# Input projections of a hybrid decoder step as seven products per pair of column blocks, in three passes over the tokens

## The chip, the cores and the metric

The kernel runs on one core of a Trainium2 chip. The metric is the device time of one execution in microseconds (us), the median of three runs. The profile shows one further execution, taken by the hardware profiler.

## The reference, cut to what matters

One layer of a decoder trunk, over 2048 prompt tokens and 8 tokens of running sequences (2056 in all), with 1024 channels, all in float32:

```python
xn = rmsnorm(x, norm_w)
proj = xn @ w_in        # 1024 x 10248
q, k, v, i_pre, f_pre, o_pre, z_m, b_g, c_g, x_c, z_c, g_m, g_c = jnp.split(proj, offs, axis=-1)
h, C1, n1, m1 = mlstm_chunkwise(q, k * DQK ** -0.5, v, ig, lf, C0, n0, m0)   # 4 heads
h = rmsnorm_per_head(h) * sigmoid(o_pre) * silu(z_m)
y_m = h @ w_proj_m
cv, conv1 = short_conv(c_g * x_c, conv0, conv_w)      # width 3, causal
y_c = (silu(z_c) * b_g * cv) @ w_proj_c
out = x + (sigmoid(g_m) * y_m + sigmoid(g_c) * y_c) @ w_out
```

and a final RMS norm. Besides the outputs for both groups of tokens the kernel returns the states of the mLSTM (C, n, m) and the last rows of the convolution.

## The kernel before, in words

Every float32 product is made of three fp32r matmuls: an operand is split into a high part (ScalarE, ACT, copies it to fp32r) and a low part (VectorE, DVE, subtracts), and high x high, high x low and low x high are summed in PSUM.

Phase A (from L128) normalises and transposes x. ACT (`hi`, L261) and DVE (`lo`, L310) split the transposed tile out of PSUM into `RH` and `RL`, which hold all 2056 tokens in SBUF; the v columns and the two gate columns are multiplied there (L365).

Phase B (from L395) makes all other input projections. It takes 36 pairs of column blocks of 128: q and k (4 pairs), o and z (8), then c and x, s and b (16 pairs, two per channel block), gm and gc (8). For each block SyncE's queue (SP) loads 1024 x 128 weights (`load_w`, L514), ACT makes `w_hi` (L751), DVE `w_lo` (L874), and TensorE (PE) runs five tiles of 412 or 410 tokens (`TILES`), each of 24 matmuls, into two PSUM banks in turn (`tile`, L1138 to L1151). ACT or DVE empties each tile (L785, L789, L803, L834, L851, L856; L943, L1035, L1060) into a row of 2056 tokens in SBUF, which SP stores to DRAM. The order of the work is written out by hand, with a semaphore for each step, and every engine's queue runs in order.

The mLSTM's 16 chunks of 128 tokens are spread over the 16 pairs of the convolution stage, one chunk to a pair. A chunk's steps are done between tiles: scores and the transposed k before tile 0 (L1201, L1205), one head before each of tiles 2 to 5 (L1217 to L1219, and on DVE L982 to L990), the normalised h transposed before tile 8 (L1223). The 8 samples' state updates follow in the gm/gc pairs (L1099 to L1108). GpSimd (POOL) does nothing but powers of a few elements (L237, L736, L738, L1603), memsets and masks.

Phases C (L1485) and D (L1675) are the three output projections; they use 294 and 512 columns per matmul. The change leaves their code as it is.

```python
for k in range(KB):
    for w, x in ((WH, g.RH), (WH, g.RL), (WL, g.RH)):
        last = nc.tensor.matmul(G[j % 2][:, 0:n], w[:, par, k, :], x[:, k, c0:c0 + n], ...)
```

Of the kernel before, what the change touches and what calls it, by code (L numbers as in the profile page):

```python
# [45 lines left out]
TILES = [(0, 412), (412, 412), (824, 412), (1236, 410), (1646, 410)]  # L46
NTILE = len(TILES)
# [39 lines left out]
def build(nc, inputs, outputs):  # L87
# [4 lines left out]
    with top:  # L92
        top.enter_context(nc.allow_non_contiguous_dma(reason="small per-channel columns"))
        RH = sbuf(nc, top, "RH", [P, KB, T], F32R)
        RL = sbuf(nc, top, "RL", [P, KB, T], F32R)
# [5 lines left out]
        g.v_rows = dram("v_rows", T, D)  # L101
        g.qT_d = dram("qT_d", NH, P, TP)
# [11 lines left out]
        g.RH, g.RL, g.RHf = RH, RL, RH[:, :, :].bitcast(F32)  # L114
# [5 lines left out]
        g.IF = sbuf(nc, early, "IF", [P, NT, 2 * NH])  # L120
        with early:
            phase_a(nc, g)
            phase_b(nc, g)
        phase_c(nc, g)
        phase_d(nc, g)


def phase_a(nc, g):  # L128
# [7 lines left out]
    xt = [sbuf(nc, ctx, f"xt{j}", [P, D]) for j in range(2)]  # L136
    stage = [sbuf(nc, ctx, f"wv_stage{j}", [P, VW]) for j in range(2)] + [g.S[:, 1], g.S[:, 0]]
# [12 lines left out]
    transposed, hi_set, lo_set = sem("transposed"), sem("hi_set"), sem("lo_set")  # L150
    v_done, v_act, v_dve = sem("v_done"), sem("v_act"), sem("v_dve")
    v_stored = [sem("v_stored0"), sem("v_stored1")]

# [10 lines left out]
    def seen(i, par):  # L164

        return 8 * i + (8 if par else 16)

# [12 lines left out]
    with nc.Block() as block:  # L180

        @block.sync
        def _(sp):
# [22 lines left out]

            def body(i, par):
                if rows(i) == P:
                    sp.wait_ge(transposed, i)
                    load_x(i + 1, 1 - par)  # L210
                if isinstance(i, int) and i == 2:
                    store(0, 0)
                store(i - 1, 1 - par)

            over_tiles(sp, body)

# [26 lines left out]

        @block.scalar
        def _(act):
# [12 lines left out]
            def hi(i):  # L258
                act.wait_ge(transposed, i + 1)
                for j in range(2):  # L260
                    nc.scalar.activation(g.RH[:, 4 * j:4 * j + 4, at(i)], turned(i)[j][:, :, 0:rows(i)], ACT.Copy).then_inc(hi_set, 1)  # L261

# [14 lines left out]
            hi(0)  # L277
            hi(1)
# [4 lines left out]
            def body(i, par):  # L283
                hi(i)
# [10 lines left out]
        def _(dve):  # L295
# [11 lines left out]
            def lo(i):  # L307
                for j in range(2):
                    dve.wait_ge(hi_set, 2 * i + j + 1)
                    nc.vector.tensor_tensor(g.RL[:, 4 * j:4 * j + 4, at(i)], turned(i)[j][:, :, 0:rows(i)],  # L310
                                            g.RHf[:, 4 * j:4 * j + 4, at(i)], ALU.subtract).then_inc(lo_set, 1)
# [18 lines left out]
            lo(0)  # L330
            lo(1)
# [5 lines left out]
            def body(i, par):  # L337
                lo(i)
# [10 lines left out]
        def _(pe):  # L349
# [11 lines left out]
            def block_product(i, j, k):  # L361

                n = rows(i)
                for m, (x, w) in enumerate(((g.RH, WH), (g.RH, WL), (g.RL, WH))):
                    last = nc.tensor.matmul(V[3 * (i % 2) + j][:n, 0:VC], x[:, k, i * P:i * P + n],  # L365
# [29 lines left out]
def phase_b(nc, g):  # L395
# [3 lines left out]
    WS = g.S[:, :, 0:D].rearrange("p a (k n) -> p a k n", k=KB)  # L399
    WH = sbuf(nc, ctx, "w_hi", [P, 2, KB, P], F32R)  # L400
    WL = sbuf(nc, ctx, "w_lo", [P, 2, KB, P], F32R)

    E0 = sbuf(nc, ctx, "row0", [P, TP])
    E1 = sbuf(nc, ctx, "row1", [P, TP])
    ZT = sbuf(nc, ctx, "z_tanh", [P, 2, 412])
    CV = sbuf(nc, ctx, "conv_tile", [P, 412])
# [4 lines left out]
    nM = sbuf(nc, ctx, "negM", [P, NH, P])  # L411
# [20 lines left out]
    ut_rows = [nM[0:2 + NS, :, :].rearrange("p a b -> p (a b)"), ZT[0:2 + NS, :, :].rearrange("p a n -> p (a n)")[:, 0:512]]  # L432
# [13 lines left out]
    G = [psum(nc, ctx, f"b_g{j}", [P, 512]) for j in range(2)]  # L446
    PS = psum(nc, ctx, "b_s", [P, NH, P])
    PT = [psum(nc, ctx, f"b_t{j}", [P, NH, P]) for j in range(2)]
    PN = [psum(nc, ctx, f"b_n{j}", [P, 512]) for j in range(2)]
    PC = psum(nc, ctx, "b_c", [P, 512])  # L450
# [1258 lines left out]
```

## Time and profile before

| what | value |
|---|---|
| three runs | 2554.98, 2556.01, 2557.18 us |
| profiled execution, its own time | 2556.17 us |
| its span in the trace | 2554.4 us |
| granted TensorE clock, mean | 0.995 |
| busy: PE, DVE, ACT, POOL | 99%, 32%, 17%, 2% of the span |
| DMA | 233.92 MB, mean 92 GB/s |

Matmuls are pipelined, so the duration in a matmul's row is longer than the distance from one start to the next; a rate is read as a window's length over its matmuls. The span holds four stretches of PE: phase A to 225.2 us, phase B from 231.1 to 1975.0 us, phase C from 1981.8 us and phase D to the end.

### The profile page before, as it was taken

To read this page: it belongs to the slowest core of one execution; us is meant where nothing else is said; L and a number is where in the kernel's file an instruction comes from. 1 tells how busy PE (TensorE), PEld (TensorE's weight loads), DVE (VectorE), ACT (ScalarE), POOL (GpSimd) and SP (SyncE) were. 2 spreads that over 40 slices of the span, in tenths; PEclk is the share of its full clock that TensorE was granted. 3 is DMA by queue.
4 is the path that set the end of the run, shared out by engine and by line. 5 is a ranking of instruction groups with operands and counts; after the bars stand their busy time and mean duration, and the time that the engine had idled before them with its cause. 6 is when DMAs were issued, how large, how long until landed. Compare 5 with 4: busy or idle time off the path is not lost. (4 is left out here: it accounts for less than half of the span.)

```text
span 2554.4 us, 35363 instructions
## 1 busy us (share of the span) xinstructions
PE 2517.9 (99%) x14265; PEld 2449.2 (96%) x14265; DVE 814.6 (32%) x1415; ACT 435.0 (17%) x806; POOL 43.5 (2%) x66
## 2 busy tenths in 40 slices
PE   7999999999999999999999999999999999999998
PEld 7998999999999999999999999999999999999886
DVE  4331000211213534535345353231212622324333
ACT  3221111111111111121111111111111301001111
POOL 0000000000000000000000000000000000000000
PEclk9999999999999999999999999999999999999999
DMA  4223122121213312233122321252333753335442
GB/s 149 83 83 62 67 82 70 33 66 33 66 33 87 91 53 78 62 91 86 54 78 70 99 70 41 72 147 91 113 109 100 258 159 101 106 94 167 128 148 84
DMA packets 238896, 233.92 MB, mean 92 GB/s; under 512 B 16010, under 2 KB 216970, under 8 KB 233862
## 3 DMA queue, kind: packets, MB, share of 16 engines
q1 hardware_dynamic: 238854, 233.33, 30.1%
q8 instruction: 31, 0.51, 0.1%
q14 instruction: 11, 0.09, 0.0%
HBM read 152.62 MB, written 80.71 MB: 91 GB/s over the span
## 5 line engine op out<-in xcount | busy, mean ns | idle before, releaser
L1148 PE MATMUL b_g<-RH,w_hi 128*128 128x412 f32 (+1 forms) x2880 | 1021.2, 355 | 5.8 <-DVE w_lo L874 5.8
L1148 PE MATMUL b_g<-RL,w_hi 128*128 128x412 f32 (+1 forms) x2880 | 1006.7, 350 | 0.0
L1148 PE MATMUL b_g<-RH,w_lo 128*128 128x412 f32 (+1 forms) x2880 | 1006.1, 349 | 0.0
L1148 PEld LDWEIGHTS b_g<-RH,w_hi 128*128 128x128 f32 x2880 | 542.0, 188 | 9.8 <-DVE w_lo L874 6.1
L1148 PEld LDWEIGHTS b_g<-RL,w_hi 128*128 128x128 f32 x2880 | 541.8, 188 | 4.2
L1148 PEld LDWEIGHTS b_g<-RH,w_lo 128*128 128x128 f32 x2880 | 541.7, 188 | 1.4
L1485 PE MATMUL c_g<-act_hi,RH 128*128 128x294 f32 x896 | 268.4, 300 | 6.7 <-DVE act_lo L1435 6.7
L1485 PE MATMUL c_g<-act_lo,RH 128*128 128x294 f32 x896 | 268.8, 300 | 0.0
L1485 PE MATMUL c_g<-act_hi,RL 128*128 128x294 f32 x896 | 268.6, 300 | 0.0
L874 DVE TENSOR_TENSOR w_lo<-stages,w_hi 128x1024 fp32r<-128x1024 f32 x72 | 88.2, 1225 | 558.8 <-ACT w_hi L751 558.6
L1485 PEld LDWEIGHTS c_g<-act_hi,RH 128*128 128x128 f32 x896 | 169.6, 189 | 7.6 <-issue 7.3
L1485 PEld LDWEIGHTS c_g<-act_lo,RH 128*128 128x128 f32 x896 | 170.1, 190 | 0.0
L1485 PEld LDWEIGHTS c_g<-act_hi,RL 128*128 128x128 f32 x896 | 170.0, 190 | 0.0
L365 PE MATMUL a_v<-wv_hi,RH 128*128 128x344 f32 (+1 forms) x408 | 133.3, 327 | 3.6 <-DVE wv_lo L315 3.2
L751 ACT ACTIVATE w_hi<-stages 128x1024 fp32r<-128x1024 f32 x72 | 76.0, 1055 | 327.8 <-PE b_g L1148 324.9
L365 PE MATMUL a_v<-wv_hi,RL 128*128 128x344 f32 (+1 forms) x408 | 131.7, 323 | 0.0
L943 DVE SCALAR_TENSOR_TENSOR row<-z_tanh,b_g 128x412 f32<-128x412 f32 (+1 forms) x80 | 46.6, 583 | 266.7 <-ACT z_tanh L778 266.7
L365 PE MATMUL a_v<-wv_lo,RH 128*128 128x344 f32 (+1 forms) x408 | 130.9, 321 | 0.0
L1675 PE MATMUL d_g<-RH,mix_hi 128*128 128x512 f32 (+1 forms) x272 | 108.7, 400 | 4.2 <-DVE mix_lo L1617 4.2
L1675 PE MATMUL d_g<-RH,mix_lo 128*128 128x512 f32 (+1 forms) x272 | 108.2, 398 | 0.0
L1675 PE MATMUL d_g<-RL,mix_hi 128*128 128x512 f32 (+1 forms) x272 | 107.7, 396 | 0.0
L778 ACT ACTIVATE z_tanh<-b_g 128x412 f32<-128x412 f32 (+1 forms) x80 | 41.1, 514 | 259.7 <-PE b_g L1148 259.7
(219 smaller groups left out, 1783.0 us busy)
## 6 DMA issues: line engine op xcount, KB each, us to landing
stages<-w_in SPq DMA_DIRECT2D x72, 512.0 KB, 6.0
act_stage<-cv_d SPq DMA_DIRECT2D x7, 1176.0 KB, 12.8
tanh_gate<-tm_d SPq DMA_DIRECT2D x7, 1176.0 KB, 6.0
tanh_gate<-tc_d SPq DMA_DIRECT2D x7, 1176.0 KB, 9.2
mix_d<-mix SPq DMA_DIRECT2D x7, 1176.0 KB, 7.1
gate_d<-row SPq DMA_DIRECT2D x8, 1028.0 KB, 5.6
cv_d<-row SPq DMA_DIRECT2D x8, 1028.0 KB, 5.2
tm_d<-row SPq DMA_DIRECT2D x8, 1028.0 KB, 4.5
```

The costliest lines, as they stand in the source:

```text
L365: last = nc.tensor.matmul(V[3 * (i % 2) + j][:n, 0:VC], x[:, k, i * P:i * P + n], w[:, k, j * VC:(j + 1) * VC], start=(k == 0 and m == 0), ...
L751: nc.scalar.activation(WH[:, par], WS[:, par], ACT.Copy).then_inc(w_hi, 1)
L778: nc.scalar.activation(ZT[:, b, 0:n], G[b][:, 0:n], ACT.Tanh, scale=0.5).then_inc(z_set, 1)
L874: nc.vector.tensor_tensor(WL[:, par], WS[:, par], WH[:, par].bitcast(F32), ALU.subtract).then_inc(w_ready, 1)
L943: nc.vector.scalar_tensor_tensor(out=E1[:, c0:c0 + n], in0=ZT[:, b, 0:n], scalar=1.0, in1=G[b][:, 0:n], op0=ALU.add, op1=ALU.mult).then_in ...
L1148: last = nc.tensor.matmul(G[j % 2][:, 0:n], w[:, par, k, :], x[:, k, c0:c0 + n], start=(step == 0), stop=(step == 3 * KB - 1))
L1485: last = nc.tensor.matmul(G[o % NB][:, 0:TN], w[:, k, c0:c0 + P], x[:, k, :], start=(k == 0 and m == 0), stop=(k == KB - 1 and m == 2))
L1675: last = nc.tensor.matmul(G[2 * par + j][:n, :], x[par][:, k, 0:n], w[:, k, j * N:(j + 1) * N], start=(step == 0), stop=(step == 3 * KB - 1))
```

## The change

In phase B a pair of column blocks and a stretch of 2n tokens are taken as a 2 x 2 by 2 x 2 block product (halves of the 1024 channels, the two column blocks, two token groups of n) and computed with seven block products instead of eight, by sums and differences of quarters. The tokens are taken in three passes with n = 260, 384 and 384; each pass goes through all 36 pairs and loads all their weights. A product is 12 matmuls of n columns; four PSUM banks take the seven products, three of them on top of an earlier one.

POOL makes four sums of 512 elements per partition for each pair. ACT and DVE split seven operands of 512 elements per pair, for the pair that comes next. ACT copies banks 0 out twice per pair, DVE adds five times. `RH` and `RL` are no longer kept in phases A and B: phase A also writes the transposed x to DRAM (`xT_d`), four quarters come back for each pass, and the seven x operands (`x_hi`, `x_lo`, one buffer each) are built anew in each pass. The activations run on whole rows after a pair's last product (`finish`). The stages are now q/k, o/z, gm/gc, convolution; chunks run in all four bodies (two pairs each) of gm/gc and, in passes 2 and 3, in the first two bodies of the convolution. The sample updates move to the q/k and o/z bodies of the second pass.

```diff
-TILES = [(0, 412), (412, 412), (824, 412), (1236, 410), (1646, 410)]
-NTILE = len(TILES)
+PASSES = [(0, 260), (512, 384), (1280, 384)]
...
                 for j in range(2):
-                nc.scalar.activation(g.RH[:, 4 * j:4 * j + 4, at(i)], turned(i)[j][:, :, 0:rows(i)], ACT.Copy).then_inc(hi_set, 1)
+                    nc.scalar.activation(RH[:, buf(i, par), 4 * j:4 * j + 4, 0:n], turned(i)[j][:, :, 0:n], ACT.Copy)
+                    raw = XR[:, par, 4 * j:4 * j + 4, :] if n == P else quarter(g, 0, 1 + j)[:, :, m - NS:m]
+                    nc.scalar.activation(raw, turned(i)[j][:, :, 0:n], ACT.Copy).then_inc(raw_set, 1)
...
+CH0 = (0, 4, 10)
+CHUNKS = (4, 6, 6)
+SEGMENTS = [
+    [("qk", 0, 1, "gates_a"), ("qk", 1, 2, "gates_b"), ("oz", 0, 4, None), ("gates", 0, 4, "chunk"),
+     ("conv", 0, 6, None), ("conv", 6, 7, "dec_first"), ("conv", 7, 8, "turn")],
+    [("qk", 0, 2, "decode2"), ("oz", 0, 4, "decode1"), ("gates", 0, 4, "chunk"), ("conv", 0, 2, "chunk"),
+     ("conv", 2, 3, "dec_last"), ("conv", 3, 7, None), ("conv", 7, 8, "turn")],
+    [("qk", 0, 2, None), ("oz", 0, 4, None), ("gates", 0, 4, "chunk"), ("conv", 0, 2, "chunk"),
+     ("conv", 2, 3, "state"), ("conv", 3, 7, None), ("conv", 7, 8, "end")]]
...
 @block.sync
+def load_w(pair, s, i, q):
+    sp.wait_ge(w_ready, 7 * pair)
+    for blk, c0 in enumerate(columns(s, i, q)):
+        sp.dma_start(RW[par][:, blk], w_in_v[:, :, bass.ds(c0, P)]).then_inc(w_in_s[par][blk], 16)
+def body(p, s, i, extra, following):
+    load_w(pair + 2, *following, 0)
...
+    load_w(pair + 3, *following, 1)
+    store_rows(p, s, i, 0)
...
...
+    store_rows(p, s, i, 1)
...
 @block.gpsimd
+def sums(pair, half, par):
+    for blk in range(2):
+        pool.wait_ge(w_in_s[par][blk], 16 * (half + 1))
+    w = RW[par]
+    pool.wait_ge(w_ready, 7 * pair + 4)
+    nc.gpsimd.tensor_tensor(SB[:, 0], w[:, 1, 0:4, :], w[:, 1, 4:8, :], ALU.add).then_inc(s_set, 1)
+    nc.gpsimd.tensor_tensor(w[:, 1, 0:4, :], w[:, 0, 0:4, :], w[:, 1, 0:4, :], ALU.subtract).then_inc(s_set, 1)
+    pool.wait_ge(s_set, 4 * pair + 2)
+    nc.gpsimd.tensor_tensor(SB[:, 1], SB[:, 0], w[:, 0, 0:4, :], ALU.subtract).then_inc(s_set, 1)
+def last_sum(pair, par):
+    pool.wait_ge(w_ready, 7 * pair + 7 + 5)
+    nc.gpsimd.tensor_tensor(w[:, 0, 4:8, :], w[:, 0, 4:8, :], SB[:, 1], ALU.subtract).then_inc(s_set, 1)
...
+last_sum(pair + 1, 1 - q)
+sums(pair + 2, half_of(p, s, i, q) + 1, q)
...
 @block.scalar
+def step(p, s, i, q, j):
+    act.wait_ge(done, 7 * pair + j + 1)
+    if j == 0:
+        nc.scalar.activation(P1[:, 0:n], G[0][:, 0:n], ACT.Copy).then_inc(x_free, 1)
+    if j == 4:
+        nc.scalar.activation(ER[:, q, 0, 0:n], G[0][:, 0:n], ACT.Copy).then_inc(x_free, 1)
+    w_high(j, pair + 1, half_of(p, s, i, q) + q, 1 - q)
+...
 @block.vector
+def step(p, s, i, q, j):
+    if j == 1:
+        nc.vector.tensor_tensor(U2[:, 0:n], P1[:, 0:n], G[1][:, 0:n], ALU.add).then_inc(ev, 1)
+    elif j == 2:
+        nc.vector.tensor_tensor(U3[:, 0:n], U2[:, 0:n], G[2][:, 0:n], ALU.add).then_inc(ev, 1)
+    elif j == 3:
+        nc.vector.tensor_tensor(ER[:, q, 1, n:2 * n], U3[:, 0:n], G[3][:, 0:n], ALU.add).then_inc(ev, 1)
+    elif j == 5:
+        nc.vector.tensor_tensor(ER[:, q, 1, 0:n], U2[:, 0:n], G[2][:, 0:n], ALU.add).then_inc(ev, 1)
+    elif j == 6:
+        nc.vector.tensor_tensor(ER[:, q, 0, n:2 * n], U2[:, 0:n], G[3][:, 0:n], ALU.add).then_inc(ev, 1)
+    w_low(j, pair + 1, 1 - q)
...
+for n, j in enumerate(RORD):
+    w_low(LEFT[n], 0, 0)
+    x_low(0, j)
...
 @block.tensor
+def product(p, s, i, q, j):
+    pe.wait_ge(w_ready, 7 * pair + 7 + j + 1)
+    if s == "qk" and q == 0:
+        pe.wait_ge(r_ready, 7 * p + RPOS[j])
...
+    elif j == 5:
+        pe.wait_ge(ev, 5 * pair + 7)
+    else:
+        pe.wait_ge(ev, 5 * pair + 8)
+    for k in range(4):
+        for m, (w, x) in enumerate(((LH, OH), (LH, OL), (LL, OH))):
+            last = nc.tensor.matmul(bank[:, 0:n], w[:, j, k, :], x[:, j, k, 0:n],
+                                    start=(j < 4 and k == 0 and m == 0), stop=(k == 3 and m == 2), skip_group_check=True)
+    last.then_inc(done, 1)
```

In `product`, j = 0 waits for ACT's copy of bank 0 in the pair before, j = 4 for P1 of this pair, 1 to 3 for adds of the pair before, 5 for U3 (the add of step 2) and 6 for the add of step 3. `store_rows(..., 1)` waits for `finish` of a body's second pair. The loop over `RORD` stands before the first pair of the first pass; in the last pair of a pass ("turn") `x_high` and `x_low` of the next pass follow the steps. In a chunk, step 0 is the scores and transposes on PE and the masked minimum on DVE, step 1 eight exponentials on ACT, step 2 the weighted scores on DVE, and PE takes the heads before products 3, 5, 7 and 9 of the body's 14.

`finish` is, on o/z: two tanh (ACT), then two scalar_tensor_tensor and a tensor_scalar (DVE); on gm/gc: two tanh; on the convolution's first pair (c, x): one multiply and a copy of two columns; on its second (s, b): one tanh, then three DVE operations; all on 2n columns. The convolution itself is three DVE operations in steps 0 to 2 of that second pair (in the first pass two more of 8 columns).

## Rows read from the trace of the kernel before

**Rows 1.** The page, part 2: busy tenths of PE and its clock, 40 slices.

```profile
PE   7999999999999999999999999999999999999998
PEclk9999999999999999999999999999999999999999
```

**Rows 2.** Windows: us, then busy us (x instructions) by engine, clock, DMA share, GB/s.

```profile
231.13:1974.95 1743.82, 1743.82 (x9401) 1724.83 (x9401) 536.04 (x990) 288.98 (x619) 22.93 (x17) 1.00 0.26 75
...
270.00:500.00 230.00, 230.00 (x1232) 229.31 (x1231) 20.42 (x20) 37.77 (x67) 0.00 (x0) 1.00 0.21 65
...
2060.00:2200.00 140.00, 140.00 (x1026) 140.00 (x1026) 45.29 (x71) 13.05 (x6) 0.00 (x0) 1.00 0.33 103
```

**Rows 3.** The page, part 5: one of phase B's three matmul groups.

```profile
L1148 PE MATMUL b_g<-RH,w_hi 128*128 128x412 f32 (+1 forms) x2880 | 1021.2, 355 | 5.8 <-DVE w_lo L874 5.8
```

**Rows 4.** Timeline of PE, 878 to 904 us: a chunk's steps between tiles (start, duration).

```profile
880.23 1.05 PE L1201 MATMUL b_s<-qT,kT 128*128 128x128 f32 x8
881.12 0.60 PE L1205 MATMUL b_t<-ident,kT 128*128 128x128 f32 x4
881.47 0.43 PE L1148 MATMUL b_g<-RH,w_hi 128*128 128x412 f32 x1
```

**Rows 5.** Groups by form, DVE: count, busy us, mean ns, idle before.

```profile
L874 DVE TENSOR_TENSOR w_lo<-stages,w_hi 128x1024 fp32r<-128x1024 f32 x72 | 88.2, 1225 | 558.8 <-ACT w_hi L751 558.6 <-DVE sample_wide L1091 0.2
L1412 DVE TENSOR_TENSOR act_lo<-act_stage,act_hi 128x2352 fp32r<-128x2352 f32 x13 | 33.9, 2608 | 22.9 <-ACT act_hi L1383 22.9
...
L1421 DVE SCALAR_TENSOR_TENSOR mix<-tanh_gate,c_g 128x294 f32<-128x294 f32 x56 | 24.7, 459 | 109.0 <-PE c_g L1485 86.9 <-DMA mix_d<-mix 22.1
...
L1035 DVE TENSOR_TENSOR row<-row,b_g 128x412 f32<-128x412 f32 x24 | 14.0, 584 | 66.1 <-PE b_g L1148 66.1
...
L972 DVE TENSOR_TENSOR q_weighted<-q_weighted,qT 128x512 f32<-128x512 f32 x16 | 10.9, 679 | 0.0
```

**Rows 6.** Groups by form, ACT.

```profile
L751 ACT ACTIVATE w_hi<-stages 128x1024 fp32r<-128x1024 f32 x72 | 76.0, 1055 | 327.8 <-PE b_g L1148 324.9 <-PEq L180 2.9
L1383 ACT ACTIVATE act_hi<-act_stage 128x2352 fp32r<-128x2352 f32 x13 | 28.3, 2174 | 257.3 <-PE c_g L1485 251.2 <-DMA act_stage<-cv_d 3.5 <-DMA act_stage<-hg_d 2.5
...
L817 ACT ACTIVATE decay<-decay,a_in 128x128 f32<-128x128 f32 x64 | 20.5, 391 | 12.4 <-DVE decay L965 12.4
```

**Rows 7.** Groups by form, POOL: its longest row and a mask.

```profile
L738 POOL TENSOR_TENSOR sample_wide<-sample_wide,minus_half 128x32 f32<-128x32 f32 x1 | 5.4, 5430 | 365.3 <-DVE sample_wide L1126 365.3
...
L730 POOL TENSOR_SCALAR_AFFINE_SELECT cum_upper<-ones 128x128 f32<-128x128 f32 x1 | 0.3, 292 | 0.0
```

**Rows 8.** DMA issues: count, KB, median us from issue to landing.

```profile
stages<-w_in SPq DMA_DIRECT2D x72, 512.0 KB, 6.0
```

**Rows 9.** Timeline, 222 to 243 us: from phase A's last matmul into phase B.

```profile
225.05 0.32 PE L365 MATMUL a_v<-wv_hi,RL 128*8 128x344 f32 x1
...
228.76 1.06 ACT L751 ACTIVATE w_hi<-stages 128x1024 fp32r<-128x1024 f32 x1 [2.91 <-PEq L180]
...
231.13 0.71 PE L1148 MATMUL b_g<-RH,w_hi 128*128 128x412 f32 x1 [5.76 <-DVE w_lo L874]
...
232.32 0.55 PE L1148 MATMUL b_g<-RH,w_hi 128*128 128x412 f32 x1
...
232.67 0.55 PE L1148 MATMUL b_g<-RL,w_hi 128*128 128x412 f32 x1
...
237.09 0.35 PE L1148 MATMUL b_g<-RH,w_lo 128*128 128x412 f32 x1
```

**Rows 10.** Timeline, 1974 to 1982 us: the end of phase B.

```profile
1974.72 0.35 PE L1148 MATMUL b_g<-RH,w_lo 128*128 128x410 f32 x1
...
1975.64 0.33 SPq L708 DMA_DIRECT2D tc_d<-row  x1
...
1981.79 0.58 PE L1485 MATMUL c_g<-act_hi,RH 128*128 128x294 f32 x1 [6.72 <-DVE act_lo L1435]
```

**Rows 11.** Group by form, ACT: the high part of x out of PSUM in phase A.

```profile
L261 ACT ACTIVATE RH<-a_tr 128x512 f32 x24 | 13.0, 596 | 4.9 <-PE a_tr L357 4.9
```

More of the change, by code:

```diff
@@ L723, in _ @@
+            sums(0, 0, 0)
+            x_difference(0)
             nc.gpsimd.memset(dec[:, 0, 0:2 * KB], 0.0).then_inc(const_set, 1)
@@ L798, in _ @@
[L798 to L811 removed]
+            act.sem_inc(x_free, 2)
@@ new lines, in body @@
+            def body(p, s, i, extra):
+                for q in range(2):
+                    for j in range(7):
+                        if extra == "chunk":
+                            chunk(chunk_of(p, s, i), 7 * q + j)
+                        if extra in ("gates_a", "gates_b"):
+                            gate_logs(14 * i + 7 * q + j)
+                        step(p, s, i, q, j)
+                        if extra == "turn" and q == 1 and j in (0, 1, 2, 3, 6):
+                            x_high(p + 1, j)
+                    finish(p, s, i, q)
+                    if extra == "turn" and q == 1:
+                        x_high(p + 1, 4)
+                        x_high(p + 1, 5)
@@ new lines, in body @@
+            def body(p, s, i, extra):
+                for q in range(2):
+                    for j in range(7):
+                        extras(p, s, i, extra, 7 * q + j)
+                        step(p, s, i, q, j)
+                        if s == "conv" and q == 1:
+                            convolve(p, i, j)
+                        if extra == "turn" and q == 1 and j in (0, 1, 2, 3, 6):
+                            x_low(p + 1, j)
+                    finish(p, s, i, q)
+                    if extra == "turn" and q == 1:
+                        x_low(p + 1, 4)
+                        x_low(p + 1, 5)
@@ new lines, in links @@
+            def links(p, s, extra):
+                n = {"oz": 2, "conv": 6 if p == 0 else 4}.get(s, 0)
+                return n + {"chunk": 3 * NH, "decode2": 6, "decode1": 3}.get(extra, 0)
+            for n, j in enumerate(RORD):
+                w_low(LEFT[n], 0, 0)
+                x_low(0, j)
+            for p in range(3):
+                for s, lo, hi, extra in SEGMENTS[p]:
+                    if hi - lo == 1:
+                        body(p, s, lo, extra)
+                    else:
+                        with dve.Fori(lo, hi) as i:
+                            own.enter(i - lo, links(p, s, extra))
+                            body(p, s, i, extra)
+                        own.leave(hi - lo)
@@ L1262, in phase_b, with body @@
+            def body(p, s, i, extra):
+                for q in range(2):
+                    for j in range(7):
+                        extras(p, s, i, extra, 7 * q + j)
+                        product(p, s, i, q, j)
+            over_segments(pe, body)
     ctx.close()
```

1343 lines of the change are left out of this document (742 added, 601 removed).

## The prediction

> **What bounds the kernel now.** I first read the page's slices [rows 1]: TensorE is busy in all of them at full clock, so a microsecond taken from its work is a microsecond of the span until another engine makes it wait. The windows [rows 2] then give phase B: 1743.8 us of the 2554.4 us span, PE busy throughout, DVE 31% and ACT 17% of it, DMA at 0.26. Nothing is waited for there. The change touches phase B, the edges of it and ACT's work in phase A; phases C and D keep their code and their time.
>
> The sum is made against the profiled execution's 2556.2 us, which is 0.2 us above the median of the three runs. A difference of 0.2% (5 us) is about what a measurement of this kernel can tell from none.
>
> **What the change takes from TensorE.** A stretch of phase B with nothing but projections holds 1232 matmuls in 230.00 us: 186.7 ns for 411 columns on average [rows 2]. Phase C holds 1026 of 294 columns in 140.00 us: 136.5 ns. The line through the two is 0.429 ns a column, so 384 columns take 175.1 ns and 260 columns 121.9 ns. The 384 lies between measured points. The 260 lies outside: it can't be under 108.3 ns (260 columns at 2.4 GHz) nor over the 136.5 ns of 294. A weight load isn't in the way at 122 ns, since four transposes, each with 128 x 128 weights of its own, start within 0.35 us, 88 ns apart [rows 4].
>
> Before: 3 x 2880 = 8640 matmuls [rows 3] x 186.7 ns = 1613.0 us. After: 36 pairs x 7 products x 12 = 3024 matmuls in each pass, 3024 x 121.9 ns + 6048 x 175.1 ns = 368.6 + 1059.0 = 1427.6 us. **That is 185.4 us less** (144 to 227 by the two ends for 260 columns). The other 128 us of phase B (chunks, small transposes, the start) remain on PE.
>
> A product lasts 1.46 us in pass 1 and 2.10 us in passes 2 and 3; a pair 10.2 or 14.7 us, where it was 45.
>
> **What it adds to the engines beside it.** Durations by length come from two rows each. DVE with two inputs: 512 elements 0.68 us, 1024 1.23, 2352 2.61 [rows 5], so 520 are 0.70, 768 0.96, 1040 1.24 and 1536 1.76. DVE with a PSUM input: 294 elements 0.46 and 412 0.58 [rows 5], so 260 are 0.42 and 384 0.55. ACT: 1024 and 2352 are 1.06 and 2.17 [rows 6], so 512 are 0.62, 1040 1.07 and 1536 1.49.
>
> A pair now costs DVE 7 x 0.68 + 5 x 0.42 = 6.9 us in pass 1 and 7.5 us later, and the convolution's body of two pairs 13.8 + 5.6 = 19.4 us against PE's 20.5 us in pass 1 (5.6: one multiply, three operations of the convolution, three of `finish`), 22 against 29.4 later. ACT has 7 x 0.62 + 2 x 0.5 + two tanh = 6.5 us a pair. Both fit, DVE in pass 1 only just.
>
> POOL's four sums of 512 elements a pair have no row of their kind. From below, DVE's 0.68 us for the same sum bounds it. From above there is only the power of 32 elements, 5.43 us [rows 7], 170 ns an element, which would make a sum 87 us. The mask, 128 elements in 0.29 us with one input [rows 7], is nearest, since it too is one simple pass; by length it gives 4 x 0.29 = 1.2 us, which I take. Four are 4.8 us a pair, under 10.2.
>
> **What gets onto the path.** Six places.
> (a) Phase A's start: ACT makes two more copies of 0.60 us [rows 11] for tile 1 before the low part can be taken: **+1 us**. Later ones hide behind products of 11 us.
> (b) The start of B. Before, PE stood 5.8 us, then ran at the lower clock level, 0.35 us a matmul, until 237.1 us [rows 9]. After, the first product needs a 1040-element x operand (+0.7 us), and DVE makes all seven operands, 7 x (0.68 + 1.24) = 13.4 us, before it takes the first sum out of PSUM. The second product waits for three POOL sums. Product 5 waits for U3, so for those 13.4 us, about 3 us lost in the POOL chain, memsets and bias adds (2 us), ACT's logarithms (2.4 us) and four more DVE operations: some 23 us after the block's start against the 12 us that PE needs with its slow start. **+11 us, +0.7, and +5 us** for a second spell at the lower clock (17 matmuls cost 2.8 us extra in the first) and the gate steps behind it: 17.
> (c) Two turns between passes. DVE's last pair of pass 1 costs 6.9 + 4.7 + 7 x 1.76 = 23.9 us; then 2.5 us to U3; PE would want product 5 of the next pair at 10.2 + 10.5 = 20.7 us. Wait 5.7. At the second turn 7.5 + 5.8 + 12.3 + 2.5 = 28.1 against 14.7 + 10.5 = 25.2: 2.9. POOL's own sums of 1536 elements and a spell at the lower clock add some 4 us: **+12 us**.
> (d) The weight feed in pass 1. SP stores a body's last row only after `finish`, 3.6 us behind PE in the convolution (0.42 + 0.68, tanh 0.6, 3 x 0.70), and only then loads the next weights: stores and two issues 2.8 us, 6.0 us to landing [rows 8], three POOL sums 3.6 us, then 1.7 us to the add that PE waits for: 17.7 us. PE is there at 10.2 + 5 x 1.46 = 17.5 us. This is at the edge, and the row stores, both weight blocks and, in gm/gc, chunk loads share the queue. I take 2 us for each of 8 convolution bodies and 1 for each of the other 8 with `finish`: **+24 us**, with 0 and 60 as its ends (60 is R1's 3.7 us in each of the 16). In passes 2 and 3 the same chain has 25 us and is hidden; if it grew past that, (d) would come three times.
> (e) Chunks. Between a chunk's scores and its first head there were two tiles, 9 us; now three products. ACT's eight exponentials, about 0.31 us apart (2.5 us), start after step 0; scores are ready 7.0 us into a pair where PE arrives after 1.2 + 4.4 = 5.6 in pass 1, and 7.6 against 7.5 later: 4 x 1.4 + 12 x 0.2 = **+8 us**.
> (f) The end of B. Before, the last store was issued 0.9 us after the last matmul's start and PE began phase C 7.1 us after that start [rows 10]. Now an add, a tanh and three DVE operations of 768 come first, 0.55 + 0.8 + 2.9: **+5 us**.
>
> Sum: 2556.2 - 185.4 + 1 + 17 + 12 + 24 + 8 + 5 = **2438 us**.
>
> DMA: two more loads of 37.7 MB of weights and about 25 MB of x raise 234 MB to some 335, near 140 GB/s, above phase B's 75 [rows 2] but with the queue's share still about half. I cost it only in (d).
>
> **The rivals.**
> *R1, a shared port.* No row of before shows POOL and DVE at wide operations together. If a POOL sum held up every DVE operation with two SBUF inputs, POOL and these would have to fit one after another: a convolution body in pass 1 has 14 x 0.68 + 5.6 - 0.5 = 14.6 us of them and 9.6 us of POOL, 24.2 against 20.5 us. 8 bodies x 3.7 = 30 us less the 16 of (d) already in, +14; DVE's wait at the other 8 bodies +6; at turns POOL's 11 us join DVE's, +12; start and chunks +4. Time 2474. The Trainium skill states just this ("SBUF — State Buffer", Who interferes with whom): DVE with two SBUF inputs and GpSimd reading SBUF exclude each other for the whole instruction. It also gives 4.5 us for a GpSimd add of 2048 float32 elements ("GPSIMD Engine Reference", 3.1), by which, as an estimate, a sum of 512 takes 1.1 us.
> *R2, cover holds.* If POOL runs nearer 0.7 us a sum and the loads land in time, (d) and half of (c) vanish: 2408.
> *R3, POOL sets the pace; slower.* PE's time per pair over the three passes is (1427.6 + 122)/108 = 14.3 us. At t a sum, POOL needs 4t. My forecast's gain of 118 us is 1.1 us a pair, so it is gone at 4t = 15.4, t = 3.9 us. At t = 4.4, 108 x 17.6 = 1901 against 1550, so 2556 - 185 + 351 + 40 = 2762. For it: the power row. Against it: the mask.
>
> **How the numbers follow.** Forecast 2438: 0.45. R1 2474: 0.33. R2 2408: 0.13. R3: 0.06. 0.03 for losses over 185 us by many small waits. Between 2408 and 2492 lie the forecast, R2's centre and R1 with half again its price; that leaves about 2 in 10 out. The forecast, R1 and R2 are all faster: 0.91; same 0.02; slower 0.07.
>
> **What would show it.** In the profile after: 9072 matmuls of phase B, with 175 ns between starts at 384 columns and 122 at 260, and the second and third pass without idle time away from turns and chunks. PE's idle time should sit in pass 1's convolution, before U3 at phase B's start (one wait of 6 us or more) and at two turns. R1 would show w_lo operations well over 0.68 us whenever POOL runs. I am wrong if a 260-column matmul takes over 136 ns, if passes 2 and 3 show waits in every pair, or if a POOL sum takes over 2 us.

## The result: 3.1% slower, and the profile after

The changed kernel takes 2634.6 us (median of 4 runs, 2633.0 to 2636.6) against 2555.5 us of the kernel before on the same chip: ratio 1.031, 95% interval 1.029 to 1.033. The forecast was 2438 us in a range of 2408 to 2492, faster. It was wrong in the sign. The profiled execution took 2633.5 us, with a span of 2631.5. Of the experiments below, one execution of three_causes took 3694.9 us at a mean granted clock of 0.58, and its ratio leaves that one out.

The page's slices of the changed kernel, against [rows 1]:

```profile
PE   7996986898868997999998898999999899999998
POOL 0003543444345443434535443343344000000000
PEclk9997998998978998999999998999999999999999
```

TensorE was never idle in phase B and at full clock; now 15 of the 40 slices are under 9 tenths busy where there were two, and 7 show a lowered clock. The windows say how much (us, then busy us and instructions of PE, PEld, DVE, ACT, POOL, clock, DMA share, GB/s): phase B whole, then its first 555 us (pass 1), then roughly passes 2 and 3, against [rows 2]:

```profile
234.50:2050.20 1815.70, 1619.58 (x9833) 1583.00 (x9833) 1448.38 (x2129) 723.03 (x1391) 784.32 (x512) 0.94 0.44 117
234.50:790.00 555.50, 450.21 (x3255) 435.27 (x3256) 453.77 (x710) 232.95 (x462) 253.86 (x172) 0.88 0.44 113
790.00:1430.00 640.00, 584.39 (x3252) 571.35 (x3250) 515.61 (x724) 244.91 (x466) 285.25 (x181) 0.97 0.47 128
1430.00:2050.00 620.00, 584.78 (x3328) 576.38 (x3328) 478.99 (x697) 245.17 (x465) 245.22 (x160) 0.98 0.42 110
```

Phase B has lengthened from 1743.8 to 1815.7 us. TensorE is idle for 196.1 us of it (105.3 in the first window), and at a mean granted clock of 0.94 its matmuls are stretched besides. Its own work, counted at full clock, did shrink, by more than forecast. Two timelines of PE, at 260 and at 384 columns (start, duration):

```profile
559.78 0.28 PE L1435 MATMUL b_g<-x_lo,w_hi 128*128 128x260 f32 x1
...
561.09 0.28 PE L1435 MATMUL b_g<-x_hi,w_hi 128*128 128x260 f32 x1
...
1499.82 0.33 PE L1435 MATMUL b_g<-x_hi,w_lo 128*128 128x384 f32 x1
...
1500.86 0.33 PE L1435 MATMUL b_g<-x_hi,w_lo 128*128 128x384 f32 x1
```

Eleven starts of 260 columns lie in 1.31 us, 119 ns each, and six of 384 in 1.04 us, 173.3 ns. So the projections are 3024 x 119 + 6048 x 173.3 ns = 1408 us of TensorE, 20 less than the 1427.6 forecast. With that number the kernel would have taken 2556.2 - 1613.0 + 1408.0 = 2351 us if nothing else had changed; **everything else has cost 283 us, where the forecast's terms (a) to (f) make 67.** Phase B holds 277 of the 283: by the same replacement it would have lasted 1743.8 - 1613.0 + 1408.0 = 1538.8 us. Of these 277, 196 are idle time and 1619.6 - 1538.8 = 81 are busy time in excess, which I put down, as an estimate, to the lowered clock: the 9833 matmuls are 9072 and the 761 others that phase B had before.

TensorE's waits by releaser (us in total, times, longest) name the places. The kernel before had none of the first five, and 5.8 us at the start of phase B [rows 3]:

```profile
PE b_g L1435 <- DVE part L1128: 67.4, 29, 8.6
PE b_s L1472 <- DMA qT<-qT_d: 38.2, 3, 13.0
PE b_s L1487 <- DVE scores L1205: 33.9, 16, 3.9
PE b_g L1435 <- DVE x_lo L1116: 22.9, 3, 9.3
PE b_g L1435 <- DVE rows L1132: 13.9, 11, 3.7
```

The first is product 5 waiting for U3, the second the k and q of the first chunk of each pass, the third a chunk's scores, the fourth the x operands at the start and the two turns. The waits are short, but behind the long ones TensorE runs at its 1.2 GHz level for a while: after the second (13.0 us), the window 415 to 416 us shows a granted clock of 0.50, and after a wait of 5.5 us near the start the window 252 to 254 us does too.

**Why VectorE is late.** Groups of VectorE and POOL by form (count, busy us, mean ns, idle before), against [rows 5, 7]:

```profile
L1110 DVE TENSOR_TENSOR w_lo<-stages,w_hi 128x512 fp32r<-128x512 f32 x270 | 263.5, 976 | 62.9 <-ACT w_hi L988 58.2
L1110 DVE TENSOR_TENSOR w_lo<-w_raw,w_hi 128x512 fp32r<-128x512 f32 x270 | 242.1, 897 | 83.5 <-ACT w_hi L988 78.7
L1134 DVE TENSOR_TENSOR rows<-part,b_g 128x384 f32<-128x384 f32 x72 | 39.8, 553 | 19.2 <-PE b_g L1435 17.6
...
L881 POOL TENSOR_TENSOR w_sums<-w_sums,w_raw 128x512 f32<-128x512 f32 x54 | 93.5, 1731 | 4.2
L888 POOL TENSOR_TENSOR stages<-stages,w_sums 128x512 f32<-128x512 f32 x54 | 73.2, 1356 | 293.4 <-DVE w_lo L1110 293.4
```

The subtraction `w_lo` was forecast at 0.68 us and has means of 0.98 and 0.90; additions that take one input from PSUM stay at the forecast 0.55. A POOL sum forecast at 1.2 us takes 1.36 us where it mostly runs alone (L888) and 1.73 where it starts beside VectorE's work. The means mix two cases. Sorting the 756 `w_lo` of the trace by whether a POOL operation of over 1.2 us overlaps them, 494 run alone, 0.69 us on average and none over 0.694, and 262 run beside one, 1.28 us on average. The timelines of VectorE and POOL at the end of pass 1 show it by single operations:

```profile
740.20 0.69 DVE L1110 TENSOR_TENSOR w_lo<-w_sums,w_hi 128x512 fp32r<-128x512 f32 x1
...
743.17 1.33 DVE L1110 TENSOR_TENSOR w_lo<-stages,w_hi 128x512 fp32r<-128x512 f32 x1
...
748.73 3.98 DVE L1159 SCALAR_TENSOR_TENSOR rows<-z_tanh,rows 128x520 f32<-128x520 f32 x1
752.75 3.80 DVE L1161 TENSOR_TENSOR conv_row<-conv_row,rows 128x520 f32<-128x520 f32 x1
756.58 0.70 DVE L1162 TENSOR_TENSOR rows<-conv_row,rows 128x520 f32<-128x520 f32 x1
```

```profile
743.92 1.74 POOL L878 TENSOR_TENSOR w_sums<-w_raw 128x512 f32<-128x512 f32 x1
...
748.22 3.94 POOL L895 TENSOR_TENSOR x_quarters<-x_quarters 128x1536 f32<-128x1536 f32 x1
752.23 3.75 POOL L897 TENSOR_TENSOR x_quarters<-x_quarters 128x1536 f32<-128x1536 f32 x1
```

L1161 and L1162 are the same kind of operation on 520 elements: 3.80 us beside POOL's 3.75, 0.70 us once POOL is done. L1161 ends at 756.55, 0.57 us after POOL's instruction (755.98). So VectorE with two inputs in SBUF did not run slower beside POOL, it waited for the end of POOL's instruction. Then TensorE waits (last field: idle time and releaser):

```profile
759.30 0.56 PE L1435 MATMUL b_g<-x_hi,w_hi 128*128 128x260 f32 x1 [8.64 <-DVE part L1128]
```

That is what the Trainium skill states ("SBUF — State Buffer", Who interferes with whom): an exclusive lock, held for the instruction. By that rule, the trace agrees.

**The unforeseen wait.** SP's timeline at the first chunk of pass 1, and TensorE's and its weight load's rows:

```profile
407.29 0.43 SPq L640 DMA_DIRECT2D gate_d<-rows  x1
409.59 0.39 SPq L685 DMA_DIRECT2D kT<-kT_d  x1
410.03 0.51 SPq L686 DMA_DIRECT2D qT<-qT_d  x1
```

```profile
413.33 1.86 PE L1472 MATMUL b_s<-qT,kT 128*128 128x128 f32 x7 [13.03 <-DMA qT<-qT_d]
```

The chunk's k and q are asked for only after the last row of the o/z stage has been stored and has landed. A chunk used to follow other chunks in one stage, one to a pair of 45 us; now the first chunk of each pass stands at the head of a stage, right behind the rows of the stage before.

### The profile page after: what moved, and what is told of

It reads as the page before. It is cut to its first block and busy times, and to the rows that moved or that the text cites. A ratio compares the mean times of both kernels' runs of the same rounds, so it can differ in the third digit from the quotient of the medians.

```text
span 2631.5 us, 43480 instructions
## 1 busy us (share of the span) xinstructions
PE 2390.0 (91%) x14697; PEld 2304.4 (88%) x14697; DVE 1734.1 (66%) x2556; ACT 885.8 (34%) x1613; POOL 812.6 (31%) x558
## 5 line engine op out<-in xcount | busy, mean ns | idle before, releaser
L1435 PE MATMUL b_g<-x_hi,w_hi 128*128 128x384 f32 (+1 forms) x3024 | 1005.3, 332 | 113.2 <-DVE part L1128 67.4
L1435 PE MATMUL b_g<-x_lo,w_hi 128*128 128x384 f32 (+1 forms) x3024 | 980.2, 324 | 0.0
L1435 PE MATMUL b_g<-x_hi,w_lo 128*128 128x384 f32 (+1 forms) x3024 | 979.7, 324 | 0.0
L1435 PEld LDWEIGHTS b_g<-x_hi,w_hi 128*128 128x128 f32 x3024 | 591.5, 196 | 128.5 <-DVE part L1128 46.7
L1435 PEld LDWEIGHTS b_g<-x_lo,w_hi 128*128 128x128 f32 x3024 | 591.8, 196 | 2.1
L1435 PEld LDWEIGHTS b_g<-x_hi,w_lo 128*128 128x128 f32 x3024 | 589.6, 195 | 0.0
L1110 DVE TENSOR_TENSOR w_lo<-stages,w_hi 128x512 fp32r<-128x512 f32 x270 | 263.5, 976 | 62.9 <-ACT w_hi L988 58.2
L1110 DVE TENSOR_TENSOR w_lo<-w_raw,w_hi 128x512 fp32r<-128x512 f32 x270 | 242.1, 897 | 83.5 <-ACT w_hi L988 78.7
L988 ACT ACTIVATE w_hi<-w_raw 128x512 fp32r<-128x512 f32 x270 | 169.4, 628 | 203.5 <-PE b_g L1435 163.6
L888 POOL TENSOR_TENSOR w_raw<-w_raw,w_sums 128x512 f32<-128x512 f32 x54 | 71.4, 1322 | 430.8 <-DVE w_lo L1110 421.0
L1110 DVE TENSOR_TENSOR w_lo<-w_sums,w_hi 128x512 fp32r<-128x512 f32 x216 | 169.8, 786 | 42.4 <-ACT w_hi L988 39.8
L1758 PEld LDWEIGHTS c_g<-act_hi,RH 128*128 128x128 f32 x896 | 169.6, 189 | 11.9 <-issue 11.8
L888 POOL TENSOR_TENSOR stages<-stages,w_sums 128x512 f32<-128x512 f32 x54 | 73.2, 1356 | 293.4 <-DVE w_lo L1110 293.4
```

Source lines behind the costliest of these rows:

```text
L888: nc.gpsimd.tensor_tensor(w[:, 0, 4:8, :], w[:, 0, 4:8, :], SB[:, 1], ALU.subtract).then_inc(s_set, 1)
L988: nc.scalar.activation(LH[:, j], w_source(j, par), ACT.Copy).then_inc(w_hi, 1)
L1110: nc.vector.tensor_tensor(LL[:, j], w_source(j, par), LH[:, j].bitcast(F32), ALU.subtract).then_inc(w_ready, 1)
L1435: last = nc.tensor.matmul(bank[:, 0:n], w[:, j, k, :], x[:, j, k, 0:n], start=(j < 4 and k == 0 and m == 0), stop=(k == 3 and m == 2), ski ...
L1758: last = nc.tensor.matmul(G[o % NB][:, 0:TN], w[:, k, c0:c0 + P], x[:, k, :], start=(k == 0 and m == 0), stop=(k == KB - 1 and m == 2))
```

## The experiments

The first theory ("port"): POOL's sums and VectorE's two-input operations hold each other up. Its rival ("latency"): the four sums follow each other, 1.5 us each, and reach the second weight block late whatever the port does; ScalarE's waits speak for it, 67.5 us in 24 waits on the third sum in pass 1 (114.8 us in 49 over the whole of phase B). Each time below is a median of at least 4 runs, with the ratio to the kernel before run beside it (2555.5 to 2556.3 us each time); differences are against 2634.6. short_sums, sums_apart, three_causes and lo_short leave out part of the sums or of the low parts, so their times are no times of the full scheme. All edits are to the changed kernel.

**short_sums and sums_apart.**

```
-  tensor_tensor(SB[:, 0], w[:, 1, 0:4, :], w[:, 1, 4:8, :], ALU.add)
+  tensor_tensor(SB[:, 0, :, 0:8], w[:, 1, 0:4, 0:8], w[:, 1, 4:8, 0:8], ALU.add)     # from pair 2 on, the other three alike
+  for k in range(4):                                                                 # sums_apart only
+      pool.wait_ge(fx, 4 * pair + k + 1)
+      tensor_tensor(FX[:, 0], FX[:, 1], FX[:, 1], ALU.add).then_inc(fx, 1)
```

> The four weight sums of a pair on POOL work on 32 of their 512 columns from pair 2 on (the values are not the scheme's then); waits and counts are as in the changed kernel. Latency theory: the four sums of a pair follow each other on POOL, 4 x 1.5 us, in a pair that in pass 1 should last 10 us, they come late at the second weight block, ScalarE and then VectorE queue behind them, and VectorE's addition that frees bank 2 is late; with short sums pass 1 loses most of its waits. Port theory: POOL's sums slow VectorE's two-input operations (w_lo 128x512 takes 0.79 to 0.98 us against 0.68 forecast), and VectorE is late on its own account. Both expect the same here: 2450 to 2500 us, phase B shorter by 130 to 180 us, ScalarE's wait for w_sums gone. If it stays above 2580, POOL has no part in it.

> As short_sums, and POOL runs four additions of 128x512 over a block of its own after each pair's sums, which nobody waits for: POOL's load and its use of SBUF are those of the changed kernel, the chain behind its sums is short. Port theory: VectorE is slowed as before, w_lo stays at 0.8 to 1.0 us, and the time stays within 40 us of the changed kernel's 2635. Latency theory: the time lies within 40 us of short_sums, 2450 to 2540.

Measured: short_sums 2517.3 us (0.984, 0.983 to 0.986), 117 us less; sums_apart 2594.9 us (1.015, 1.014 to 1.017), 40 us less. The first is 17 us above the range that both theories gave; the second is at the very edge of the port's (within 40) and outside the latency's. Neither theory holds alone: taking POOL's chain off the path while its load stays gives 40 us, taking the load away gives another 78. So the load is two thirds of it and the chain one. The load of sums_apart sits at one fixed place of the pair, so the split is approximate. What is left in short_sums (two windows: phase B, and its first pass; then VectorE and POOL rows):

```profile
236.50:1933.60 1697.10, 1577.14 (x9832) 1550.00 (x9833) 1219.38 (x2129) 725.88 (x1391) 283.28 (x512) 0.97 0.47 126
236.50:710.40 473.90, 418.56 (x3240) 408.45 (x3241) 360.32 (x704) 233.29 (x459) 96.22 (x169) 0.93 0.50 130
```

```profile
L1110 DVE TENSOR_TENSOR w_lo<-w_raw,w_hi 128x512 fp32r<-128x512 f32 x270 | 187.2, 693 | 130.0 <-ACT w_hi L988 124.1
...
L922 POOL TENSOR_TENSOR h<-h,sumsq 128x1024 f32<-128x1024 f32 x16 | 30.4, 1902 | 1.3
```

`w_lo` from `w_raw` is back at 0.69 us and from `stages` at 0.75; from `w_sums` it stays at 0.79. Product 5's wait falls from 67.4 to 15.8 us. Two things show in the windows. Phase B is 118 us shorter, of which 76 are idle time and 42 are busy time at the same matmuls, so the clock's share came back too. And from the first projection matmul of a pass to that of the next, the three passes take 474, 623 and 601 us where they took 552, 653 and 611: 78 us of the gain lie in pass 1, 30 in pass 2 and 10 in pass 3.

**sum_order.**

```
   sum 1, sum 2 of pair n+2
+  last_sum(pair n+1)            # was ahead of sum 1
   sum 3 of pair n+2
```

> Only the order on POOL is changed: the first two sums of pair n+2 go ahead of the last sum of pair n+1, so that the chain starts one product earlier (at the fourth w_lo of the pair, not at its fifth). Same work, same load. Latency theory: the third sum is 1.4 us (pass 1) to 2.1 us earlier in every pair, ScalarE's wait for w_sums of 67.5 us in pass 1 (24 waits) falls below 35 us, and the kernel is 30 to 80 us shorter. Port theory: no less load, less than 15 us.

Measured 2695.7 us (1.054, 1.053 to 1.056), 61 us **more**: the expectation had the wrong sign, by either theory. POOL's and ScalarE's rows:

```profile
L878 POOL TENSOR_TENSOR w_sums<-stages 128x512 f32<-128x512 f32 x54 | 72.2, 1338 | 492.4 <-DMA stages<-w_in 295.6 <-DVE w_lo L1116 196.1 <-DVEq L1103 0.6
```

```profile
ACT w_hi L994 <- POOL w_raw L890: 219.3, 39, 12.3
ACT w_hi L994 <- POOL stages L890: 213.8, 51, 9.4
```

The third sum's wait is gone (3.8 us), but sum 1 of pair n+2 now stands in the queue waiting for weights that are still on their way (295.6 us on this row, 27.8 in the changed kernel), and the last sum of pair n+1 waits behind it; ScalarE waits 433 us for it. The weight feed of step (d) is real and bites in all passes as soon as something is queued behind it.

**early_kq.**

```
   # SP, last oz body, before store_rows(p, s, i, 0)
+  wait for the rows issued so far; load_kq(CH0[p]); load_m(CH0[p]); load_v(CH0[p])
```

> The loads of the first chunk of each pass (k, q, the weights row and v) are issued at the start of the last oz body instead of after its last stored row. It tells the theories apart only in that it takes out what neither speaks of: three waits of TensorE on qT from its transfer, 13.0 + 12.5 + 12.6 us. Expected of both: these three are gone, 34 to 45 us less than the changed kernel, 2590 to 2600; more, up to 60, if the fall of the clock behind each of them goes too.

Measured 2603.5 us (1.019, 1.017 to 1.020), 31 us less, of an expected 34 to 45. TensorE's wait on qT is gone from the waits; the scores' wait rose from 33.9 to 42.8 us, so part came back one step later.

**dve_sums and dve_last.**

```
-  nc.gpsimd.tensor_tensor(...)         # four sums of a pair; dve_last: the last alone
+  nc.vector.tensor_tensor(...)         # behind the additions of products 5 and 6
```

> All four weight sums of a pair move from POOL to VectorE, behind the additions of products 5 and 6. Port theory: a 128x512 op with two inputs in SBUF takes VectorE 0.69 us alone and POOL 1.4 us, and they do not overlap; so VectorE gives 4 x 0.69 = 2.8 us a pair and gets back what it now waits for POOL (w_lo means of 976 and 897 ns return to about 690, some 125 us over the run), and the four sums are ready without a hop. In passes 2 and 3 (14.6 us a pair, VectorE then at some 11 to 13) it gains, in pass 1 (10 us a pair, VectorE at 9.7 before the finishing work) it is the bound and loses. Expected 2560 to 2640, pass 1 slower than in the changed kernel, passes 2 and 3 faster. Rival (VectorE's own load is the whole trouble, POOL harmless): 298 us more on VectorE, over 2700.

> Only the last sum of each pair moves to VectorE (between the addition of product 5 and the fifth w_lo); POOL keeps three. The chain on POOL starts one sum later and is 1.5 us shorter, POOL's load falls by a quarter, VectorE's rises by 0.69 us a pair and falls by what it waited for that sum. Expected 2585 to 2620 (25 to 50 us less than the changed kernel), ScalarE's wait for w_sums in pass 1 under 25 us. If VectorE's load alone counts: 2640 or more.

Measured: dve_sums 2595.4 us (1.015, 1.014 to 1.017), 39 us less; dve_last 2635.9 us (1.031), no change. dve_sums gives VectorE 4 x 108 more operations and is faster, so the load of VectorE alone, the rival in that expectation (over 2700 us), is refuted. `w_lo` falls to 732 and 700 ns, as the port theory has it; but the move also takes the hop through POOL away, so the 39 us are not the port's alone. That pass 1 would lose was wrong: between 235 and 790 us TensorE gets through 3359 matmuls, where it did 3255.

```profile
235.00:790.00 555.00, 459.90 (x3359) 445.83 (x3360) 465.89 (x884) 240.98 (x472) 42.52 (x27) 0.90 0.45 116
```

dve_last failed its expectation. With three sums left on POOL, `w_lo` from `stages` still takes 990 ns, and the moved sum itself 1019: as long as POOL runs sums of this size, an operation moved to VectorE waits for the ones that stay. That this is why nothing was gained is argued from these means and was not tested.

**lo_short.**

```
-  tensor_tensor(LL[:, j], w_source(j, par), LH[:, j], ALU.subtract)
+  tensor_tensor(LL[:, j, 0:1], w_source(j, par)[:, 0:1], LH[:, j, 0:1], ALU.subtract)   # from pair 2 on
```

> VectorE's low parts of the weights are formed for one of four contraction blocks (the others keep an old value), POOL's sums stay as they are. Port theory (each engine waits for the other's operation): VectorE's load falls by some 5 us a pair to below POOL's, POOL's sums return from 1.3 to 1.7 us to about 1.3 us, and the waits of product 5 go: 2500 to 2540, near short_sums. Theory that POOL's chain of four sums alone is the bound: still over 2590.

Measured 2553.9 us (0.999, 0.998 to 1.000), 81 us less: outside both numbers, nearer to the port's. POOL's sums keep to 1.32 to 1.48 us. VectorE's operations of 128 elements have means of 377 to 522 ns and a median of 293 ns, so some of them wait for POOL even so. Relieving either side of the pair helps, POOL's more (117 against 81). This run takes VectorE's own load away along with its hold on POOL, so it does not tell the two apart.

**balanced, combined.**

```
-PASSES = [(0, 260), (512, 384), (1280, 384)];  CH0 = (0, 4, 10); CHUNKS = (4, 6, 6)
+PASSES = [(0, 324), (640, 384), (1408, 320)];  CH0 = (0, 5, 11); CHUNKS = (5, 6, 5)   # and the stages' tables to match
```

> Passes of 324, 384 and 320 columns instead of 260, 384 and 384, with 5, 6 and 5 chunks: same products, same sums and same VectorE operations in number, but no pair lasts 10 us (12.4, 14.6 and 12.2). If pass 1 loses 160 us because four POOL sums and seven w_lo do not fit in 10 us, the loss falls to the level of pass 2 (some 80 us), pass 3 gains a little less than it gave (from 40 to 60): 2570 to 2600. If the loss is of each stage's waits and not of the pair's length, 2620 to 2640.

> balanced, early_kq and dve_last in one. If the three are separate causes their gains add: about -31 (measured), -35 and -50 from 2635: 2520, between 2500 and 2560. Above 2570 they share a cause.

Measured: balanced 2602.9 us (1.018, 1.017 to 1.020), 32 us less, of an expected 35 to 65; combined 2576.8 us (1.008, 1.007 to 1.010), which is the 31 and 32 us of the two parts that had given something, and nothing from dve_last (2571.6 if they add). By its expectation, over 2570 meant a shared cause; the dve_last run, which gave nothing alone, explains the miss better. The shortness of pass 1 is a cause, but making the passes more equal gives back only 32 us.

**conv_late and heads_late.**

```
-  convolve(p, i, j)                         # behind products 0, 1, 2
+  convolve(p, i, j - 2)                     # conv_late: behind 2, 3, 4
-  elif at in (3, 5, 7, 9):                  # heads of a chunk
+  elif at in (4, 6, 8, 10):                 # heads_late
```

> The three steps of the convolution run behind products 2, 3 and 4 of the second pair of a conv body instead of behind 0, 1 and 2; same work. If product 5 waits for U3 (67.4 us in all) because VectorE has the convolution to do before it, the waits at q=1, j=5 of the conv bodies go (3.3 to 8.8 us in each of the eight of pass 1): 2600 to 2615. If U3 is late from POOL's sums through the second w_lo, no more than 10 us.

> The four heads of a chunk run one product later (products 4, 6, 8, 10 instead of 3, 5, 7, 9). TensorE's wait for the scores, 33.9 us in 16, goes; VectorE has 2 us more for them. Expected 2600 to 2612; if VectorE's lag at that place is carried to the next step the wait moves to the head norm at product 13 and the time stays within 8 us of 2635.

Measured: conv_late 2641.7 us (1.033, 1.031 to 1.035), 7 us more, with 70.4 us of waits on U3: the convolution's place is not what makes U3 late, and that expectation's first branch fell. heads_late 2616.5 us (1.024, 1.023 to 1.026), 18 us less, between its two expectations: the wait for the scores has left the list of the largest and 19.0 us in 16 waits on POOL's normalised h (L922) came in its place.

**three_causes.** short_sums, early_kq and heads_late in one.

> Short sums on POOL (32 of 512 columns, from pair 2 on), the early loads of k and q, and the heads one product later, in one kernel. Alone they took 118, 31 and 18 us off the changed kernel's 2635. If they are separate causes: 2463 to 2475, within 37 us of the forecast of 2438, and the forecast's miss of 197 us is mostly told. If they share time (a stall taken away by one was hidden behind another): 2490 or more.

Measured 2471.8 us (0.967, 0.965 to 0.969). The sum of the three alone is 2634.6 - 117 - 31 - 18 = 2468. They add to within 4 us, so they are separate causes.

```profile
234.50:1885.40 1650.90, 1570.73 (x9831) 1545.42 (x9832) 1215.22 (x2130) 724.76 (x1391) 292.47 (x512) 0.98 0.48 129
```

TensorE's idle time in phase B is 80 us here against 196, and its busy time is 1570.7 - 1538.8 = 32 us over the full-clock estimate, against 81.

**best and best_conv.** balanced, early_kq, dve_sums and heads_late, with and without conv_late.

> early_kq, balanced, dve_sums, conv_late and heads_late together. Gains measured so far against the changed kernel: 31, 32 and 39 us; 25 each expected of the last two. If they add: 2490; if the balanced passes and the sums on VectorE take from each other (VectorE then has 10.1 us and more of work in a pair of 12.2 us): 2530 to 2560. Above 2560 there is a bound that none of these runs has touched.

> best with the convolution's steps back behind products 0, 1 and 2. Alone, moving them cost 6 us of 2635. If that holds here too: 2498 to 2505. If the later place pays once VectorE makes the sums: 2510 to 2520.

Measured: best 2507.5 us (0.981, 0.979 to 0.983), best_conv 2508.2 us (0.981, 0.979 to 0.983). They compute all that the kernel before computes, and beat it by 1.9% and the changed kernel by 4.8%. Where the convolution's steps stand makes no difference. The gains add, to within 8 us: 2634.6 - 31 - 32 - 39 - 18 = 2515. What is left on TensorE in best (us in total, times, longest):

```profile
PE b_g L1453 <- DVE x_lo L1118: 22.1, 3, 12.5
PE b_t L1511 <- POOL h L907: 21.6, 16, 2.8
PE b_g L1453 <- DVE part L1130: 18.5, 12, 5.0
PE b_g L1453 <- DVE rows L1134: 11.5, 5, 3.8
```

## Why the prediction was wrong

**TensorE's work**: right, and 20 us better than forecast, since 384 columns took 173.3 ns against 175.1, and 260 took 119 against 121.9.

**The step that failed** is the costing of POOL's sums and what hangs on it: "it gives 4 x 0.29 = 1.2 us, which I take. Four are 4.8 us a pair, under 10.2", with (d) at 24 us and "In passes 2 and 3 the same chain has 25 us and is hidden". The sum alone takes 1.36 us (L888) and 1.73 beside VectorE, four some 6.2 us a pair; but 0.5 us a sum is not the error. The error is to compare each engine's load with TensorE's pair, one engine at a time. In 106 of the 108 pairs at least one `w_lo` takes over 0.72 us; in 49 places ScalarE waits for the third sum, 24 of them in pass 1; and TensorE waits 29 times for U3, 21 of them in pass 1. Passes 2 and 3 were not free of it either: the short sums give back 30 and 10 us there. With the sums short the kernel is 117 us faster, against 24 in (d). That the addition of U3 comes late behind both the port and the chain is what sums_apart and short_sums show together. A second term was missing with it: (d) had no price for the clock, and 42 of phase B's 118 us are busy time.

**R1**, given 0.33, was right in kind: `w_lo` operations "well over 0.68 us whenever POOL runs" are in the trace. Its place was largely right too: in the 16 convolution pairs of pass 1 short_sums takes 190.5 us where the changed kernel takes 237.2, 47 of the 118. Its price was half of what was needed: with the 24 of (d) it charges POOL's sums with 60 us, and they cost 117. It compared the summed occupancy of the two engines with the pair (24.2 against 20.5 us) in pass 1, let passes 2 and 3 hide it but for the turns (+12 there, on top of (c)'s 12), and took nothing for the clock. sums_apart against short_sums puts the load alone at 78 us. That a chain with a due time in each product can be late without a full engine is the likely reason for the rest, and is argued. R2 and R3 did not come: the sums' means are 1.32 to 1.73 us, and POOL is busy 784 of phase B's 1816 us.

**A wait not in the sum**: the loads of the first chunk of each pass, 38.2 us of TensorE's waits, 31 us by early_kq. Step (e) looked at a chunk's inner steps and took its inputs as ready. By the rule that (d) uses (SP stores a body's last row and only then loads), this could have been read from the code.

**(e)** 8 us forecast, 33.9 us waited, 18 us gained by heads_late. Its working took 0.68 us for each `w_lo` and scores ready at 7.0 us against 5.6 in pass 1 and 7.6 against 7.5 later; the 1.4 us became 3.0 a chunk and the 0.1 became 1.8. Short sums left 29.1 us of it, so POOL's sums are a small part of its cause; the rest was not isolated.

**(b)** 17 us forecast for the start of B. TensorE waits 9.3, 2.3, 5.5, 6.3 and 2.9 us there, 26.3 in all and 20.5 more than the 5.8 of before, and has a granted clock of 0.50 from 252 to 254 us, so (b) was too low by at least 3.5 us. The single wait of 6 us or more on U3 did not come as such: at that point the 6.3 us are put down to `f_log`. No run took the start apart. **(c)** 12 us forecast for the turns. The waits on x operands there are 22.9 - 9.3 = 13.6 us, but TensorE also waits for U3 in the last two pairs before each turn, 8.64 us at 759.30 as shown above and:

```profile
779.95 0.56 PE L1435 MATMUL b_g<-x_hi,w_hi 128*128 128x260 f32 x1 [7.96 <-DVE part L1128]
...
1412.98 0.41 PE L1435 MATMUL b_g<-x_hi,w_hi 128*128 128x384 f32 x1 [4.70 <-DVE part L1128]
1432.80 0.41 PE L1435 MATMUL b_g<-x_hi,w_hi 128*128 128x384 f32 x1 [3.45 <-DVE part L1128]
```

That makes 24.8 us more, 38 in all: (c) had the wait behind the turn and missed the one ahead of it, where for the first of the four POOL's x sums of 3.9 and 3.75 us stand in VectorE's way, as the rows at 748 to 756 us show. Short weight sums leave much of it (4.2, 6.0, 1.5 and 3.4 us at the same four places). **(f)** 5 forecast: from the start of the last matmul (2049.96 us) to phase C (2061.78) are 11.8 us against 7.1 [rows 10], +4.7. Right, though the terms given for it, 0.55 + 0.8 + 2.9, make 4.3. **(a)** Phase A's last work and B's start (234.54 - 9.30 = 225.2 us) stand where they stood (225.4): the +1 was not seen.

**Slips in the working.** With 136.5 ns for 260 columns the gain is 413 + 1059 against 1613, 141 us and not 144; (d)'s 0.42 + 0.68 + 0.6 + 3 x 0.70 are 3.8 us and not 3.6. Neither moves the forecast by more than 3 us.

**The falsifiers.** A 260-column matmul over 136 ns: no at full clock (119 ns); at the lower level, after phase B's start, the starts are 217 ns apart. A POOL sum over 2 us: 8 of 432, and no group's mean. Waits in every pair of passes 2 and 3: no, the two passes together wait 8 times at most at any one place outside the chunks. So none of the three was met as it was meant, and the forecast still fell; the miss went through the case given 0.03, losses over 185 us by many small waits.

**The account.** Of the 283 us, 117 are POOL's sums, 31 the first chunks' loads, 18 the scores, and 2471.8 - 2351 = 121 are left. The forecast's (a), (b), (c) and (f) make 35 of these. The other 86 are not settled as to cause. By kind, the 121 are 80 us in which TensorE is idle in phase B, some 32 of busy time in excess (a mean clock of 0.98 over 1650.9 us is worth at most 33), and 9 outside phase B. The 80 us of waits lie at the two turns (22.9), at POOL's norm (18.8), at the start (14.0) and, for the rest, at `rows`, the scores and v. No experiment took the start of phase B, the turns, POOL's norm or VectorE's `finish` apart.

## What to carry over

When sums move to GpSimd to spare VectorE, add the two engines' SBUF-to-SBUF work and treat it as one engine's, and check due times as well as loads: moving all four sums *back* to VectorE was faster though VectorE then had 432 more operations. A kernel whose TensorE is never idle has no slack to show in its profile; a scheme that cuts the work between waits to a quarter (45 us a pair to 10) needs every load, store and hop re-timed, the first of each loop above all. Waits must be priced with the clock that they cost: here 196 us of idle time went with some 81 us of slower matmuls. And a queue entry that waits for a transfer must not stand ahead of one that is ready (sum_order: +61 us).

## What the runs showed of the hardware

- A VectorE operation of 520 elements with both inputs in SBUF took 3.80 us beside a POOL operation of 3.75 us and 0.70 us after it; an addition of 384 elements with one input in PSUM has means of 546 to 554 ns in the changed kernel and all its variants, with POOL's sums or without.
- POOL's addition of two float32 rows takes 1.34 us for 512 elements (sum_order) and 2.37 us for 1040 ahead of phase B, which makes, as an estimate, 1.95 ns an element and 0.34 us. That the fit had to be made from the changed kernel is why the forecast's 1.2 us, from a mask, stood on so little.
- Short waits cost clock as well. In the first window, with 105 us of idle time in pieces, the mean granted clock is 0.88; the kernel before has 1.00 over its whole phase B [rows 2]. The 81 us of excess busy time in phase B are the estimate of its part; no run isolated it, and taking 38 us of waits away in early_kq gave 31.
